# Up projections of a two-layer MLP as seven half products (Strassen), weight sums made by accumulating transfers

## The reference

```python
D_MODEL = 2048
D_FF = 4 * D_MODEL
...
h = rmsnorm(x, g[2])
f = jnp.square(jax.nn.relu(h @ mlp_w1[i])) @ mlp_w2[i]
x = x + rmsnorm(f, g[3])
```

## Time and profile before

| | |
|---|---|
| median of 3 runs | 2350.91 us |
| span of the profiled execution, first to last instruction | 2350.0 us |
| TensorE matmuls, busy share | 2336.6 us, 99% |
| VectorE, ScalarE, GpSimd busy | 1303.4, 1081.5, 29.6 us |
| bytes moved by DMA | 446.07 MB, 190 GB/s in the mean |

### The profile page before, as it was taken

One profiled execution on the slowest core, in us unless ns is written; L12 is line 12 of the kernel. 1 busy time (PEld: TensorE's weight loads), 2 busy tenths in 40 slices (PEclk: granted clock), 3 DMA queues, 4 the chain that ended last, 5 costly groups with the idle time before them and its releaser, 6 DMA issues.

```text
span 2350.0 us, 25306 instructions
## 1 busy us (share of the span) xinstructions
PE 2336.6 (99%) x10945; PEld 1932.3 (82%) x10945; DVE 1303.4 (55%) x1330; ACT 1081.5 (46%) x1174; POOL 29.6 (1%) x48
## 2 busy tenths in 40 slices
PE   9999999999999999999999999999999999999998
PEld 7778788888888888888888888888888888888887
DVE  6665855644554544556864444544454575556664
ACT  6344444644344353444565444344344364344443
POOL 0000000000000000000000000000000010000000
PEclk9999999999999999999999999999999999999999
DMA  8445455555555555555555555555555555644444
GB/s 326 159 163 180 179 197 197 202 192 187 189 208 187 196 180 196 187 189 197 215 197 180 196 182 194 189 187 192 186 194 183 195 182 203 253 161 144 144 158 146
DMA packets 64159, 446.07 MB, mean 190 GB/s; under 512 B 7241, under 2 KB 7572, under 8 KB 12527
## 3 DMA queue, kind: packets, MB, share of 16 engines
q1 hardware_dynamic: 61568, 429.58, 51.8%
q0 software_dynamic: 2336, 14.76, 1.8%
q10 hardware_dynamic: 144, 0.12, 0.0%
HBM read 442.33 MB, written 2.10 MB: 189 GB/s over the span
## 4 chain that ended last, share of the span: by engine, by line
PE 96%; DMA 2%; ACT 1%; DVE 1%; issue 0%; ACTq 0%; POOLq 0%; POOL 0%; SPq 0%
PE P L342 93%; PE P L345 3%; DMA raw<-in_w_z 1%; ACT hi L485 0%; DVE raw_r L605 0%; DMA raw<-in_w_d 0%; DMA raw<-in_w_i 0%; ACT EV L511 0%; DVE R_h L592 0%; ACT R_h L481 0%; DVE X L592 0%; ACT EV L481 0%; DVE st L592 0%; ACT X L481 0%; DVE R_f_r L589 0%
## 5 line engine op out<-in xcount | busy, mean ns | idle before, releaser
L605 DVE TENSOR_TENSOR raw_r<-raw,hi 128x2048 fp32r<-128x2048 f32 (+3 forms) x417 | 911.9, 2190 | 930.9 <-ACT hi L485 929.6
L342 PE MATMUL P<-hi,R_h 128*128 128x512 f32 (+2 forms) x3840 | 1225.1, 393 | 2.5 <-DVE raw_r L605 1.6
L485 ACT ACTIVATE hi<-raw 128x2048 fp32r<-128x2048 f32 (+3 forms) x417 | 763.3, 1833 | 989.8 <-DMA raw<-in_w_d 387.4
L342 PEld LDWEIGHTS P<-hi,R_h 128*128 128x128 f32 x3840 | 720.5, 188 | 154.9 <-issue 8.4
L342 PE MATMUL P<-hi,R_f_r 128*128 128x512 f32 x2480 | 777.5, 391 | 0.5 <-DVE raw_r L605 0.4
L342 PE MATMUL P<-raw_r,R_h 128*128 128x512 f32 (+2 forms) x1920 | 744.7, 388 | 0.0
L342 PEld LDWEIGHTS P<-hi,R_f_r 128*128 128x128 f32 x2480 | 465.6, 188 | 97.4 <-DVE raw_r L605 0.9
L342 PE MATMUL P<-raw_r,R_f_r 128*128 128x512 f32 x1240 | 482.7, 389 | 0.0
L342 PEld LDWEIGHTS P<-raw_r,R_h 128*128 128x128 f32 x1920 | 361.0, 188 | 73.1 <-issue 4.3
L342 PEld LDWEIGHTS P<-raw_r,R_f_r 128*128 128x128 f32 x1240 | 232.9, 188 | 47.4
L589 DVE TENSOR_TENSOR R_m<-P,R_m 128x512 f32<-128x512 f32 x112 | 71.8, 682 | 0.0
(11 more groups left out here) (193 smaller groups left out, 769.5 us busy)
## 6 DMA issues: line engine op xcount, KB each, us to landing
raw<-in_w_u SPq DMA_DIRECT2D x128, 1024.0 KB, 4.8
raw<-in_w_d SPq DMA_DIRECT2D x128, 1024.0 KB, 4.8
raw<-in_w_z SPq DMA_DIRECT2D x46, 1024.0 KB, 4.8
raw<-in_w_i SPq DMA_DIRECT2D x36, 1024.0 KB, 4.8
raw<-in_w_mo SPq DMA_DIRECT2D x16, 1024.0 KB, 4.9
raw<-in_w_o SPq DMA_DIRECT2D x16, 1024.0 KB, 4.8
raw<-in_w_mkv SPq DMA_DIRECT2D x8, 1024.0 KB, 4.8
R_g<-in_rows POOLq DMA_DIRECT2D x6, 1024.0 KB, 5.6
```

The lines of the kernel that those rows point to most:

```text
L342: return self.e.matmul(o, l, r, start=start, stop=stop, skip_group_check=True)
L485: self.e.activation(hi, raw, ACT.Copy).then_inc(*self.inc("high_made", ("high", k, d)))
L605: self.e.tensor_tensor(low, raw, hi.bitcast(f32), ALU.subtract).then_inc(*self.inc("low_made", *names))
```

## The change

In each of the 14 chunks the up projection is made as seven products of half matrices, where it took eight. `h` is seen as 2 x 2 parts of 128 positions by 1024 channels (left and right are channels, top and bottom positions), the chunk of `mlp_w1` as 2 x 2 parts of 1024 channels by 512 columns. A half product multiplies one part or sum of parts of `h` with one part or sum of parts of the weights: two tiles, 12 matmuls each. Between two half products stands one tile of down(e-1).

- The four sums of `h` (`sum_of`, `parts_of`) are made on VectorE and ScalarE during up(0), once per MLP.
- The sums of weights are made by transfers that add in place. Two buffers `chain` hold a running sum of weight parts: SyncE loads B11, then GpSimd's queue adds B12, B22 and B21 to it one after the other (`CHAIN`), each after VectorE has taken the low part of the state before. One more sum, B12 + B22, is made in two landing buffers by a load and an adding transfer (`add_tile`). Per chunk this makes 8 adding transfers of 1 MB (6 on the chain, 2 in landing buffers).
- The seven results are combined on VectorE (`combine`), with a copy on ScalarE for two of them, before the relu.
- `hi` and `low` are now buffers of their own (`NO` = 3 each), apart from 3 landing buffers; a landing buffer is free once VectorE has made `low`, an operand buffer half by half as TensorE uses it. All splits of the program are made in two halves of 128 x 1024.
- `FH`/`FL` have one copy instead of two. The gain row and the rows of the memory move to other buffers. The descriptor scratch of GpSimd's queue is set to 8192.

```diff
-NS = 4
+NL = 3
+NO = 3
 AHEAD = 2
+CHAIN = (0, 4, 6, 2)
...
-        self.raw, self.low = zip(*(both(f"raw{i}", 2048) for i in range(NS)))
-        self.hi = [sb(f"hi{i}", 2048, f32r) for i in range(NS)]
+        self.raw = [sb(f"raw{i}", 2048) for i in range(NL)]
+        self.hi = [sb(f"hi{i}", 2048, f32r) for i in range(NO)]
+        self.low = [sb(f"low{i}", 2048, f32r) for i in range(NO)]
...
-        self.FH = [v3(R_fr[:, 4096 * k:4096 * k + 2048], 8) for k in range(2)]
-        self.FL = [v3(R_fr[:, 4096 * k + 2048:4096 * k + 4096], 8) for k in range(2)]
+        self.FH, self.FL = v3(R_fr[:, 0:2048], 8), v3(R_fr[:, 2048:4096], 8)
+        self.chain = [R_f[:, 4096:6144], R_f[:, 6144:8192]]
...
+        self.SH = [None, v3(R_sr[:, 0:1024], 8), v3(R_gr[:, 2048:3072], 8), self.HH[:, 0:8, 128:256], v3(R_gr[:, 0:1024], 8)]
+        self.SL = [None, v3(R_sr[:, 1024:2048], 8), v3(R_gr[:, 3072:4096], 8), self.HL[:, 0:8, 128:256], v3(R_gr[:, 1024:2048], 8)]
+        self.S_sum = [None] + [v3(R_m[:, 1024 * n:1024 * n + 1024], 8) for n in range(4)]
...
+    def add_tile(self, k, o, i, l):
+        self.wait_ge(("loaded", k))
+        self.e.dma_start(o, i, accum_op=ALU.add).then_inc(*self.landed(f"sum{l % NL}", ("tile sum", k)))
...
+    def chain_add(self, j, o, i, free, done):
+        self.wait_ge(free)
+        self.e.dma_start(o, i, accum_op=ALU.add).then_inc(*self.landed(f"added{j}", done))
...
+    def split_part(k, d, n):
+        name, _, parts, c, kind, more, l, o = plan[k]
+        width = c // n
+        q, lows = slice(width * d, width * d + width), [("low", k, 4 // n * d + z) for z in range(4 // n)]
+        if kind == "chain":
+            raw, ready = m.chain[more[3]], ("chained", *more)
+        else:
+            raw, ready = m.raw[l % NL], ("tile sum", k) if kind == "sum" else ("loaded", k, 2 * d // n) if k < 2 else ("loaded", k)
+        free = None
+        if o >= NO:
+            free = "used", user[o - NO], 2 * d // n if plan[user[o - NO]][3] == c else 1
+        E.split(k, d, m.hi[o % NO][0:parts, q], raw[0:parts, q], m.low[o % NO][0:parts, q], ready, free, *lows)
+        if d == n - 1:
+            user[o] = k
+            if kind == "chain":
+                link(*more, ("low", k, 3))
+            else:
+                freed[l] = ("low", k, 3)
+                load_ahead()
+    def link(mlp_, e, s, j, free):
+        s, e = (s + 1) % 4, e + (s == 3)
+        i, done = 8 * e + CHAIN[s] + j, ("chained", mlp_, e, s, j)
+        if e == 8:
+            chain_last[j] = free
+        elif s == 0:
+            E.chain_load(j, m.chain[j], a[f"w_u{mlp_}"][i], free, done)
+        else:
+            E.chain_add(j, m.chain[j], a[f"w_u{mlp_}"][i], free, done)
...
+        def both_ways(e, up_banks, down_banks):
+            b11, b12, b21, b22 = ([8 * e + n + j for j in range(2)] for n in (0, 4, 2, 6))
+            plain = lambda b: [(i, "load") for i in b]
+            linked = lambda s: [(8 * e + CHAIN[s] + j, "chain", (l, e, s, j)) for j in range(2)]
+            added = [(b12[j], "sum", b22[j]) for j in range(2)]
...
+            def second(b, done):
+                k = ev(hold=True)
+                c11 = combine(k, P[b][:, :], EV[ks[1]][:, :], ALU.add, [done, ms[1]], ev_free[k])
+                bank_free[b] = [c11]
+                ks[11] = k
+                ms[11] = relu_square(k, EV[k][:, :], 0, c11, None)[1]
+                ms[1] = c11
...
+            def sixth(b, done):
+                ms[1] = combine(ks[1], P[b][:, :], EV[ks[1]][:, :], ALU.add, [done, ms[1]])
+                bank_free[b] = [ms[1]]
+                c12 = combine(ks[12], EV[ks[12]][:, :], EV[ks[1]][:, :], ALU.subtract, [ms[12], ms[1]])
+                ms[12] = relu_square(ks[12], EV[ks[12]][:, :], 0, c12, None)[1]
+                ms[1] = c12
...
+            up(1, 0, HH[:, HLEFT, TOP], HL[:, HLEFT, TOP], h_left, linked(0), first)
+            down(0)
+            up(2, 1, HH[:, HRIGHT, TOP], HL[:, HRIGHT, TOP], h_right, plain(b21), second)
+            if e == 1:
+                flush()
+            down(1)
+            up(5, 0, SH[1], SL[1], s_m[1], linked(1), fifth)
+            down(2)
+            up(3, 1, SH[4], SL[4], s_m[4], plain(b22), third)
+            down(3)
+            up(6, 0, SH[2], SL[2], s_m[2], linked(2), sixth)
+            down(4)
+            up(7, 1, SH[3], SL[3], s_m[3], added, seventh)
+            down(5)
+            up(4, 0, HH[:, HRIGHT, BOTTOM], HL[:, HRIGHT, BOTTOM], h_right, linked(3), fourth, True)
+            left_free = down(6)
+            right = [(c, *turned(c, right_ks(), right_ms())) for c in (4, 6)]
...
-    nc = bacc.Bacc("TRN2", target_bir_lowering=False, num_devices=1)
+    nc = bacc.Bacc("TRN2", target_bir_lowering=False, num_devices=1, dynamic_dma_scratch_size=8192)
```

More of the change, by code:

```diff
@@ L345, in tr, with product @@
         return self.e.transpose(o, i, self.m.ident[0:i.shape[0], 0:i.shape[0]])
[L347 removed]
+    def product(self, o, h, l, wh, wl, j, k, first, end, x_ready, free, *done):
         self.wait_ge(x_ready)
@@ L1038, in split_ahead @@
             k = at_["high"]
-            name, _, parts, c = plan[k]
-            if name not in WHOLE:
-                E.split(k, 0, m.hi[k % NS][0:parts, 0:c], m.raw[k % NS][0:parts, 0:c], m.low[k % NS][0:parts, 0:c])
+            o = plan[k][7]
+            if o is not None:
+                if o >= NO and o - NO not in used:
+                    return
+                split_part(k, 0, 2)
+                split_part(k, 1, 2)
             at_["high"] += 1
@@ L1050, in quarter, with take @@
             if not listing:
-                _, _, parts, c = plan[k]
-                q = slice(c // 4 * d, c // 4 * d + c // 4)
-                E.split(k, d, m.hi[k % NS][0:parts, q], m.raw[k % NS][0:parts, q], m.low[k % NS][0:parts, q], True)
+                split_part(k, d, 4)
         return quarter
-    def take(name):
+    def take(name, i=None, kind="load", more=None):
         j = at_["take"]
@@ L1470, in conduct @@
             first_column(4 * g + c)
-            q = slice(512 * c, 512 * c + 512)
-            E.split(g, c, m.hi[g][:, q], m.raw[g][:, q], m.low[g][:, q], True)
-    at_["high"] = 0 if listing else 4
+            if g < NO and not listing:
+                split_part(g, c, 4)
+    at_["high"] = 0 if listing else NO
     fl = {}
@@ new lines, in parts_of, with half_product @@
+        def parts_of(n, *free):
+            s_m[n] = plain_parts(SH[n], SL[n], SUM[n], [s_m[n], list(free)])
+        def half_product(b, xh, xl, ready, tiles, end, soon):
+            for n, tile in enumerate(tiles):
+                j, wh, wl = take(up_w, *tile)
+                wh, wl = v3(wh, 4), v3(wl, 4)
+                for k in range(4):
+                    x = ready[4 * n + k] if isinstance(ready, list) else ready
+                    whose = ([("product", j, 1)] if k == 3 else []) + ([("used", j, k // 2)] if k % 2 else [])
+                    E.product(P[b][:, :], xh[:, 4 * n + k, :], xl[:, 4 * n + k, :], wh[:, k, :], wl[:, k, :], j, k,
+                              n == k == 0, n == 1 and k == 3, x, bank_free[b], *whose)
+                if n == 1 and soon:
+                    end(b, ("product", j, 1))
+                release(j, ("product", j, 1))
+                if n == 1 and not soon:
+                    end(b, ("product", j, 1))
+                step()
+            return ("product", j, 1)
@@ new lines, in down_tile @@
+        def down_tile(e, i, banks, middle):
+            g, q = i // 2, i % 2
+            while None in f_m[4 * q:4 * q + 4]:
+                step()
+            j, wh, wl = take(down_w)
+            wh, wl = v3(wh, 4), v3(wl, 4)
+            for k in range(4):
+                kk = 4 * q + k
+                for t in range(2):
+                    whose = ([("product", j, t)] if k == 3 else []) + ([("used", j, k // 2)] if t == 1 and k % 2 else [])
+                    E.product(P[banks[t]][:, :], FH[:, kk, 128 * t:128 * t + 128], FL[:, kk, 128 * t:128 * t + 128], wh[:, k, :], wl[:, k, :],
+                              j, k, q == k == 0, q == 1 and k == 3, f_m[kk], bank_free[banks[t]], *whose)
+                if k == 1:
+                    middle()
+            done = ("product", j, 1)
+            release(j, done)
+            if q == 1:
+                for t in range(2):
+                    summed(e, t, g, banks[t], done)
+            step()
+            return done
@@ L1751, in mlp @@
+        first_up()
+        last_pair = nxt["pair"]
+        up_banks, down_banks = [last_pair ^ 2, (last_pair ^ 2) + 1], [last_pair, last_pair + 1]
         for e in range(1, 8):
-            up(e)
             if at is not None:
-                at(e, x_m)
-            down(e - 1)
-        out_of, squares_of = down(7)
+                at(e, None)
+            up_done = both_ways(e, up_banks, down_banks)
+        row_m.append(side_load("gain", m.gain_row, a["rows"][row].partition_broadcast(128), chain_last[0]))
```

(15 more changed lines are left out.)

266 lines of the change are left out of this document (180 added, 86 removed).

## The result

The changed kernel took 2439.99 us (median of 4 runs, 2433.57 to 2447.7) beside 2351.06 us before: a ratio of 1.038, 95% interval 1.036 to 1.040. It is 89 us slower, where the forecast was 2288 us. The span of the profiled execution is 2431.7 us.

What follows compares the result with a forecast made beforehand. TensorE's number of matmuls was taken as the bound: span 2350.0 - 76.4 removed + 8 + 5 allowed = 2286.6, with 0.9 us for the median 2288 us, 2.7% faster; 8-in-10 range 2274 to 2450 us.

Steps and rivals of the forecast that it cites:

- What was removed: Up projection: 168 matmuls for 192 per chunk, 5.46 us less each, 76.4 us over 14 chunks, all on TensorE's path.
- VectorE and ScalarE: Added splits and combinations: VectorE 66.6 us and ScalarE 55.1 us per chunk of 83.5, hidden by TensorE if order allows.
- The allowances: Work still showing: 0.6 us per chunk, 8 us in all, plus 5 us for first up projections and the start.
- The price of an add: DMA engines: 5.15 us per adding transfer, two pressed tiles' worth, between bounds of 2.58 and 9.0 us.
- The step that failed: DMA in chunks: 82.4 us of transfers in 83.5, asked for early, lateness absorbed by 8 to 10 us of split lead.
- just covered: Pair's sum in landing buffers: load 4.8, add 8.7, split 3.3, together 16.8 us, within three landings' 17.9 us.
- the chain's latency: Rival on chain adds: deciding above 24 us to land; 5 us more costs 280 us, 2550; shares 0.09 with VectorE late.
- The rival of the DMA engines as the bound: Chain and pair transfers cost more than matmuls give, from 5.97 or 5.12 us per add; 2449 to 2687 us; chance 0.27.
- transfers bind a little: Rival in chunks: adds at 4.8 to 5.9 us make a chunk 84 to 88.5 us, total 2281 to 2344; chance 0.21.

Runs made afterwards that it cites:

- The kernel without adds: The change with all 112 adding transfers made plain loads, so the sums of weights are left out: 2290.57 us, ratio 0.9744.
- the best version: The change with four landing buffers, half-tile operand buffers and product 7 second instead of sixth, except in each MLP's first chunk: 2317.74 us, ratio 0.9853.
- the 77 us that the order gives alone: The change with product 7 second and product 2 sixth, except in each MLP's first chunk, still three landing buffers: 2362.68 us, ratio 1.0053.
- the last kernel: The kernel with four landing buffers and product 7 second, with that order now also in each MLP's first chunk: 2317.34 us, ratio 0.9853.
- the nine kernels of the table: The change and eight of its follow-up variants, those with TensorE idle 55.7 to 134.4 us against 13.4 before: 2331.59 to 2440.53 us.
- the kernel with the sums on VectorE: The change with product 7 second and its pair loaded plainly and summed on VectorE, three landing buffers: 2387.64 us; same summed on GpSimd: 2428.13.

## Why the prediction was wrong

The measured 2440 us lies inside the range of 2274 to 2450 that was given, but near its upper end, which stood there for a dearer add; 0.61 had gone to a faster kernel, and the cause was another.

**What was removed.** Right: 336 matmuls fewer, 76.4 us. The kernel without adds gets it.

**VectorE and ScalarE.** Right. The half tile that the trace of before didn't have, forecast at 1.22 and 1.05 us:

```profile
L614 DVE TENSOR_TENSOR low<-R_f,hi 128x1024 fp32r<-128x1024 f32 x224 | 264.5, 1221 | 94.1 <-ACT hi L495 92.4
...
L495 ACT ACTIVATE hi<-R_f 128x1024 fp32r<-128x1024 f32 x224 | 227.7, 1052 | 100.6 <-DMA R_f<-in_w_u 66.4
```

The allowances, 8 us for what shows and 5 for the start, 13 in all, stand against 24.7 - 13.4 + 3.7 = 15.0 us of idle time (over that of before) and time at the lower clock in the run without adds. Over a chunk of 83.4 us VectorE is busy there for 64.0 us and ScalarE for 54.4, where 66.6 and 55.1 were forecast.

**The price of an add.** Right. 5.15 us was taken between 2.58 and 9.0; the change shows 5.30, the best version 5.14. In the change it is 5.30/2.71 = 1.96 times a plain tile, in the best version 2.0. The 1.93 that the Trainium skill gives for a reducing transfer ("Collectives: The Full Stack", section "The bandwidth ceiling: the fold count and why AG ≠ RS ≠ AR") is close to these rows, though it speaks of collectives and these are loads into SBUF. No run here shows what inside the transfer doubles the price.

**The step that failed** is the sentence after the sum: that three landing buffers and two chains have the transfers asked for early, and that a late one first eats the 8 to 10 us by which splits run ahead, so that little of it comes onto the path. It took 82.4 us of transfers in 83.5 us for a sum over a chunk, as if they were spread evenly over it. In its place the runs show a chunk of 94.4 us with one chain add that lands after 25.8 us, 119.2 us of idle time of TensorE and 52.3 us at the lower clock; the 8 to 10 us of lead do not cover that. Two things were on the page and not put together:
- The pair had been found "just covered", 16.8 us of 17.9. But the 16.8 us took an add at 8.7 us, the landing of one alone. In the change the adds land after 7.8 us at the least, 11.9 in the median on the chain, and 27.1 at the most. A term computed for an idle machine was used in a place where the sum above had just said that the machine is full.
- GpSimd's queue was named as holding everything in order, but not walked through. The pair of product 7 stands directly before the chain's step for product 4, so a late pair puts four adds behind each other: 4 x 5.3 = 21.2 us, and a down tile or two of 2.7 us beside them, 23.9 to 26.6 us as an estimate where 25.8 are seen.

The rival "the chain's latency" had the mechanism and the limit right: it decides from 24 us, and the eleven long landings that the chain by time shows up to 1700 us took 24.5 to 27.1. It had only a part of the 0.09 that it shared with VectorE, because of landing rows taken from a machine at half load. Its price was too high (20 us per chunk, one delay for each of four states): one state of a chunk is late, and a chunk takes 94.4 - 83.5 = 10.9 us more than forecast.

**The rival of the DMA engines as the bound** had more of the chance and is not what happened. At the 2.71 us that a load takes in the change it decides from (88.97 - 16 x 2.71)/8 = 5.70 us per add, and the add takes 5.30. The share is 0.91 and not 1 in the slow kernel, and the full load at 0.99 in the fast one. Nor is it "transfers bind a little": the transfers' sum of 85.8 us lies in that rival's 84 to 88.5, but by it a chunk would have taken 85.8 us and the kernel been some 44 us faster. Of the 10.9 us by which the chunk is too long, at most 2.3 can be the sum.

How the 145.1 us between the forecast span (2286.6) and the measured one (2431.7) came about: 105.8 us of idle and 52.3 us at the lower clock, less the 13 allowed. Lateness is shown to be the cause of the idle time by the version that keeps all transfers and moves two things. That idle time brings slow matmuls is shown below in two stretches. Not settled is how much of the lateness is the group of four and how much that of the down tiles and of the pair by itself, and how the 77 us that the order gives alone are shared between fewer stalls for `R_m` (52.7 to 10.8 us) and a better spread of the other transfers, since the group of four is still in that kernel.

## What to carry to other kernels

A sum of transfers that just fits into a period says nothing of the largest wait in it: lay the transfers out in the order of their queues, with the landing time of a machine as full as the sum says, and look for the place where the dearest ones are due together. An in-order queue that waits for one landing can turn a late transfer into a group, and the last of the group then lands late: here after 24 to 27 us, against 11.9 in the median. Check the order of the work and the number of landing buffers together; here either alone gave 77 or 21 us, and both 122.

## What the runs showed of the hardware

**An adding transfer** from HBM into SBUF costs the DMA engines 5.1 to 5.3 us per MB tile when they are nearly full (share 0.91 to 0.99), twice a plain one (2.57 to 2.71). Its issue costs GpSimd more as well: 0.86 us, against 0.53 for a plain load of the same shape, both where they stand alone.

**A stall of TensorE can be paid a second time in the clock.** In the last kernel an 11.45 us gap ends at 479.86 us. The columns are those of the earlier trace rows:

```profile
480.00:486.00 6.00, 6.00 (x15) 4.69 (x16) 1.23 (x1) 1.62 (x2) 0.00 (x0) 0.53 0.00 0
486.00:492.00 6.00, 6.00 (x28) 4.93 (x27) 3.67 (x3) 4.01 (x5) 0.86 (x1) 1.00 0.73 199
```

For 6 us the granted clock is at 0.53, near the lower of its two levels (1.2 of 2.4 GHz), and 15 matmuls fit where 28 do afterwards. In the change, the stretch of 910 to 920 us, in which TensorE stands for 4.5 us and then works, shows 0.83. In the nine kernels of the table that idle over 40 us more than the kernel before, the time at the lower clock is 0.35 to 0.52 of the added idle time (52.3 of 105.8 in the change, 44.2 of 121.0, 14.9 of 42.3). Whoever had priced the waits of these kernels by their length alone would have priced them too low by that much.

**GpSimd as an adder**: a half tile of 128 x 1024 takes it 2529 ns, where VectorE's subtraction of the same shape takes 1221 in the median. Beside GpSimd's sums a single such subtraction took up to 5531 ns, and all that read landing buffers together 62.6 us more than in the kernel with the sums on VectorE (941.9 for 879.3).
